# Two hybrid layers on one core: accumulate in PSUM, use ACT's own SiLU and GELU, and normalise one softmax on ACT

## The reference

```
def hybrid_layer(x, ...):
    z = rms_norm(x, norm1_g) @ w_in                    # 1024 -> 9984
    ya = silu(ga) * group_norm(retention(rotary(q), rotary(k), v)) * gn_g
    u  = a * sigmoid(gate)                             # conv branch
    yb = silu(layer_norm(causal_depthwise_conv31(u, conv_w) + conv_b))
    u, v = split(gelu(zc)); yc = u * (ws @ layer_norm(v) + b_s)
    p  = softmax over [scores + bias, sink]            # 8 heads of 64, window 128
    yd = p @ v
    mix = sum_n sigmoid(gate_n) * (y_n @ w_branch[n])  # 4 branches, 512 -> 1024
    x  = x + mix @ w_out
    gt, up = split(rms_norm(x, norm2_g) @ w_ffn_in)    # 1024 -> 2 x 2816
    return x + (silu(gt) * up) @ w_ffn_out
```

## Time and profile before

| | us |
|---|---|
| median of 3 runs | 2426.42 (2425.41 to 2430.86) |
| the profiled execution, its own time | 2424.03 |
| its span, first to last instruction | 2422.7 |
| PE busy | 2232.2 |
| DVE busy | 1631.0 |
| ACT busy | 1193.9 |
| POOL busy | 877.8 |

### The profile page before, as it was taken

How to read it: one execution, slowest core, us unless ns; L and a number is a source line. 1 busy time by engine, 2 the same in 40 slices (tenths; PEclk the granted TensorE clock), 3 DMA queues, 4 the chain that set the end, 5 groups by cost and what they waited for, 6 DMA issues and landing times.

```text
span 2422.7 us, 38114 instructions
## 1 busy us (share of the span) xinstructions
PE 2232.2 (92%) x15186; PEld 2068.3 (85%) x15186; DVE 1631.0 (67%) x2519; ACT 1193.9 (49%) x2040; POOL 877.8 (36%) x477
## 2 busy tenths in 40 slices
PE   8888889999999789999997798999999699898999
PEld 8887879999999678888886697889988588787997
DVE  6768742778544986666658789586655968777664
ACT  5546444454444975554552454535444255545443
POOL 5554457777200950000034474440004546442000
PEclk9999999999999999999998898899999899999999
DMA  6443445655556026666653344345664435334665
GB/s 222 131 122 112 133 152 178 183 162 179 179 185 184 12 76 194 192 194 195 194 175 126 121 144 131 105 141 163 184 190 145 131 106 156 112 116 150 183 186 160
DMA packets 102931, 369.59 MB, mean 153 GB/s; under 512 B 11362, under 2 KB 13794, under 8 KB 102116
## 3 DMA queue, kind: packets, MB, share of 16 engines
q1 hardware_dynamic: 102756, 367.15, 49.3%
HBM read 364.49 MB, written 2.62 MB: 152 GB/s over the span
## 4 chain that ended last, share of the span: by engine, by line
PE 62%; DVE 28%; ACT 5%; issue 3%; DMA 2%; POOL 1%; SPq 0%; DVEq 0%; ACTq 0%
PE stream_bank L530 10%; PE stream_bank L531 10%; PE stream_bank L532 10%; PE side_bank L530 9%; PE side_bank L531 9%; PE side_bank L532 9%; DVE conv_out L2030 6%; DVE first_hot L1970 2%; DVE unit_lo L1568 2%; DVE experts L1960 2%; ACT unit_hi L1048 1%; PE side_bank L592 1%; DVE S L1638 1%; DVE gates L1673 1%; POOL unit_lo L2302 1%
## 5 line engine op out<-in xcount | busy, mean ns | idle before, releaser
L2302 POOL TENSOR_TENSOR unit_lo<-raw,unit_hi 128x1024 fp32r<-128x1024 f32 (+1 forms) x305 | 754.0, 2481 | 519.1 <-ACT unit_hi L1048 518.8
L1048 ACT ACTIVATE unit_hi<-raw 128x1024 fp32r<-128x1024 f32 (+1 forms) x678 | 707.2, 1045 | 189.9 <-PE side_bank L532 82.6
L1568 DVE TENSOR_TENSOR unit_lo<-raw,unit_hi 128x1024 fp32r<-128x1024 f32 x373 | 459.3, 1232 | 390.6 <-ACT unit_hi L1048 390.0
L530 PE MATMUL stream_bank<-hT_hi,unit_hi 128*128 128x256 f32 x1672 | 501.4, 300 | 7.4 <-DVE unit_lo L1568 6.9
L531 PE MATMUL stream_bank<-hT_lo,unit_hi 128*128 128x256 f32 x1672 | 483.3, 289 | 0.0
L532 PE MATMUL stream_bank<-hT_hi,unit_lo 128*128 128x256 f32 x1672 | 482.5, 289 | 0.0
L530 PEld LDWEIGHTS stream_bank<-hT_hi,unit_hi 128*128 128x128 f32 x1672 | 332.2, 199 | 17.2 <-DVE unit_lo L1568 7.3
L531 PEld LDWEIGHTS stream_bank<-hT_lo,unit_hi 128*128 128x128 f32 x1672 | 331.9, 198 | 2.1
L532 PEld LDWEIGHTS stream_bank<-hT_hi,unit_lo 128*128 128x128 f32 x1672 | 330.9, 198 | 0.0
L530 PE MATMUL stream_bank<-h2T_hi,unit_hi 128*128 128x256 f32 x1152 | 327.4, 284 | 2.6 <-DVE unit_lo L1568 2.5
L531 PE MATMUL stream_bank<-h2T_lo,unit_hi 128*128 128x256 f32 x1152 | 326.7, 284 | 0.0
(11 more groups left out here) (354 smaller groups left out, 4260.6 us busy)
## 6 DMA issues: line engine op xcount, KB each, us to landing
raw<-in_peer_u_dram SPq DMA_DIRECT2D x128, 512.0 KB, 3.6
raw<-in_peer_v_dram SPq DMA_DIRECT2D x128, 512.0 KB, 3.6
raw<-in_gate_dram SPq DMA_DIRECT2D x64, 512.0 KB, 3.6
raw<-in_gt_dram SPq DMA_DIRECT2D x44, 512.0 KB, 3.6
raw<-in_up_dram SPq DMA_DIRECT2D x44, 512.0 KB, 3.7
raw<-in_ffn_out_dram SPq DMA_DIRECT2D x44, 512.0 KB, 4.2
raw<-in_branch_dram SPq DMA_DIRECT2D x32, 512.0 KB, 3.6
raw<-in_w_gate_dram SPq DMA_DIRECT2D x24, 512.0 KB, 3.6
```

Of the source, the lines that this page charges most:

```text
L530: mm(out, l.hi, r.hi, start=start, stop=False)
L1048: activation(k.unit_hi[n % SPLIT_SLOTS][:, 0:w], k.raw[n % RAW_SLOTS][:, 0:w], ACT.Copy).then_inc(k.sem("unit_hi"), 1)
L1568: V.tensor_tensor(k.unit_lo[s][:, 0:w], k.raw[n % RAW_SLOTS][:, 0:w], k.unit_hi[s][:, 0:w], ALU.subtract).then_inc(unit_lo, 1)
L2302: G.tensor_tensor(k.unit_lo[s][:, 0:w], k.raw[n % RAW_SLOTS][:, 0:w], k.unit_hi[s][:, 0:w], ALU.subtract).then_inc(k.sem("unit_lo_pool"), 1)
```

## The change

- **Convolution taps.** The sum so far is kept in `side_bank`4, in one half of the bank for even groups and the other for odd ones; only the last tap writes `cv` in SBUF. The factor one half of the gate's sigmoid moves into the 124 columns of taps (one small instruction a layer).
- **Rotation.** The product with the sines is written back into its bank; the add reads it there. The chunks use `side_bank`3 and 2 in turn, and the bank is given back after the add, one round later. `rope_tmp2` isn't used any more.
- **Gate products.** For three of the four branches the product stays in its stream bank and the add reads it there.
- **SiLU and GELU.** The evictions of `ga`, `gv` and `gu` apply ACT's function, the convolution's SiLU is one ACT instruction with the layer norm's scale and bias; the polynomials, tanh steps and multiplies go, and with them some rounds in which the side generators only waited.
- **Softmax of the window attention.** DVE stops after the inverse; ACT multiplies by it.

The diff, cut to its core:

```diff
 # PE: head
-        pe.wait_ge(k.sem("normed"), s.number + 1)
+        if s.kind == "swa":
+            pe.wait_ge(k.sem("normed_act"), s.number - HEADS_MIXER + 1)
+        else:
+            pe.wait_ge(k.sem("normed"), s.number + 1)
...
 # PE: retention
-                bank = take(SIDE + 3, (name("rot"), c))
+                bank = take(SIDE + 2 + (c + 1) % 2, (name("rot"), c))
...
 # ACT: head
+        if s.kind == "swa":
+            act.wait_ge(k.sem("inverse"), s.number - HEADS_MIXER + 1)
+            for i, (a, kn) in enumerate(s.where):
+                last = activation(s.S[:, a:a + kn], s.S[:, a:a + kn], ACT.Identity, scale=s.den[:, i:i + 1])
+            last.then_inc(k.sem("normed_act"), 1)
...
 # ACT: convolution
-                activation(k.t2[:, 0, :], k.cv[:, i, :], ACT.Tanh, scale=0.5).then_inc(k.sem("conv_tanh"), 1)
-                act.wait_ge(k.sem("conv_silu"), KM * l + i + 1)
-                split_hi(k.ys.hi[:, 4 + i, :], k.cv[:, i, :], "conv_hi", 0.5)
+                own.then(activation(k.cv[:, i, :], k.cv[:, i, :], ACT.Silu, scale=k.col(name("cln_g"), i),
+                                    bias=k.col(name("cln_b"), i)))
+                split_hi(k.ys.hi[:, 4 + i, :], k.cv[:, i, :], "conv_hi")
...
 # ACT: main
-                evict(name("ga"), i, k.ga[:, i, :])
+                evict(name("ga"), i, k.ga[:, i, :], ACT.Silu)
...
-                    evict_token_major(name("gv"), k.gv, 512)
+                    evict_token_major(name("gv"), k.gv, 512, ACT.Gelu_apprx_tanh)
...
 # DVE: head
-        own.then(V.reciprocal(s.den, s.den))
-        for i, (a, kn) in enumerate(s.where):
-            last = V.tensor_scalar(s.S[:, a:a + kn], s.S[:, a:a + kn], s.den[:, i:i + 1], None, ALU.mult)
-        last.then_inc(k.sem("normed"), 1)
+        if s.kind == "swa":
+            V.reciprocal(s.den, s.den).then_inc(k.sem("inverse"), 1)
...
 # DVE: convolution
-                cv = k.cv[:, i, :]
-                own.then(V.tensor_scalar(cv, k.cu[:, i, 0:TOKENS], w(0), k.col(name("conv_b2"), i), ALU.mult, ALU.add))
+                sums = bank[:, i % 2 * TOKENS:(i % 2 + 1) * TOKENS]
+                own.then(V.tensor_scalar(sums, k.cu[:, i, 0:TOKENS], w(0), k.col(name("conv_b2"), i), ALU.mult, ALU.add))
                 for j in range(1, TAPS2 - 1):
-                    own.then(V.scalar_tensor_tensor(cv, k.cu[:, i, j:j + TOKENS], w(j), cv, ALU.mult, ALU.add))
+                    own.then(V.scalar_tensor_tensor(sums, k.cu[:, i, j:j + TOKENS], w(j), sums, ALU.mult, ALU.add))
...
-                gelu_cubic(tmp, u, "gelu_u_cubic")
-                yield
-                yield
-                dve.wait_ge(k.sem("gelu_u_tanh"), n)
-                own.then(V.scalar_tensor_tensor(u, tmp, 1.0, u, ALU.add, ALU.mult))
...
 # DVE: retention
-                V.tensor_tensor(k.rqk[:, c, :], k.rqk[:, c, :], k.rope_tmp2[:, :], ALU.add).then_inc(k.sem("rotated"), 1)
-                dve.wait_ge(k.sem("rotated"), 8 * l + c + 1)
+                V.tensor_tensor(k.rqk[:, c, :], k.rqk[:, c, :], turned(c), ALU.add).then_inc(k.free[SIDE + 2 + (c + 1) % 2], 1)
...
+                dve.wait_ge(k.sem("rot_mm"), 8 * l + c + 1)
+                own.then(V.tensor_tensor(turned(c), turned(c), k.ret_sin, ALU.mult))
                 if c:
                     add(c - 1)
-                dve.wait_ge(k.sem("rot_mm"), 8 * l + c + 1)
-                V.tensor_tensor(k.rope_tmp2[:, :], k.bank[SIDE + 3][:, 0:TOKENS], k.ret_sin, ALU.mult).then_inc(
-                    k.free[SIDE + 3], 1)
-                dve.wait_ge(*k.over[name("rot"), c])
...
 # DVE: main, branches
-                    gated_sum(gate, k.bank[k.bank_of[label]], label, 2)
+                    product = k.bank[b][:, :].rearrange("p (a t) -> p a t", a=2)
...
-                    if 0 < place < BRANCHES2 - 1:
-                        own.then(V.tensor_tensor(total, total, gate, ALU.add))
+                    if place == 0:
+                        gated_sum(gate, k.bank[b], label, 2)
+                    else:
+                        dve.wait_ge(unit_mm, U[label] + 1)
+                        own.then(V.scalar_tensor_tensor(product, gate, 1.0, product, ALU.add, ALU.mult))
+                        V.tensor_tensor(total, total, product, ALU.add).then_inc(k.free[b], 1)
+                        dve.wait_ge(*k.over[label])
```

More of the change, by code:

```diff
@@ L1060, in evict, with evict_token_major @@
         activation(dst, k.bank[b][:, 0:TOKENS], func, **kw).then_inc(k.free[b], 1)
-    def evict_token_major(key, dst, width):
+    def evict_token_major(key, dst, width, func=ACT.Copy):
         for t in range(TILES):
             act.wait_ge(unit_mm, at.unit)
-            activation(dst[:, t, :], k.bank[SIDE + t][:, 0:width], ACT.Copy).then_inc(k.free[SIDE + t], 1)
+            activation(dst[:, t, :], k.bank[SIDE + t][:, 0:width], func).then_inc(k.free[SIDE + t], 1)
     def norm_stats(name, x, ready, junk):
@@ L1427, in retention_head @@
                 yield
[L1428 to L1431 removed]
             yield
             act.wait_ge(*k.over[name("ret_turn"), h])
[L1434 removed]
+            split_hi(k.ys.hi[:, h, :], k.ga[:, h, :], "ret_hi")
             yield
@@ L1498, in main @@
             for i in range(KM):
-                evict(name("gu"), i, k.gu[:, i, :])
+                evict(name("gu"), i, k.gu[:, i, :], ACT.Gelu_apprx_tanh)
                 yield
@@ L1635, in head @@
             dve.wait_ge(*k.over[label])
-        own.then(V.reciprocal(s.den, s.den))
-        for i, (a, kn) in enumerate(s.where):
-            last = V.tensor_scalar(s.S[:, a:a + kn], s.S[:, a:a + kn], s.den[:, i:i + 1], None, ALU.mult)
-        last.then_inc(k.sem("normed"), 1)
+        if s.kind == "swa":
+            V.reciprocal(s.den, s.den).then_inc(k.sem("inverse"), 1)
+        else:
+            own.then(V.reciprocal(s.den, s.den))
+            for i, (a, kn) in enumerate(s.where):
+                last = V.tensor_scalar(s.S[:, a:a + kn], s.S[:, a:a + kn], s.den[:, i:i + 1], None, ALU.mult)
+            last.then_inc(k.sem("normed"), 1)
         yield
@@ L2001, in layer @@
             pass
-        own.then(V.memset(k.cu[:, :, 0:TAPS2 - 1], 0.0))
+        V.memset(k.cu[:, :, 0:TAPS2 - 1], 0.0)
+        taps = k.col(name("conv_w2"), 0, TAPS2 * KM)
+        own.then(V.tensor_scalar(taps, taps, 0.5, None, ALU.mult))
         if l == 0:
@@ L2022, in convolution @@
         def convolution():
+            bank, mean, var = k.bank[SIDE + 4], k.t2[:, 0, :], k.t2[:, 1, :]
             for i in range(KM):
@@ L2033, in convolution @@
                 j = TAPS2 - 1
-                V.scalar_tensor_tensor(cv, k.cu[:, i, j:j + TOKENS], w(j), cv, ALU.mult, ALU.add).then_inc(
+                V.scalar_tensor_tensor(k.cv[:, i, :], k.cu[:, i, j:j + TOKENS], w(j), sums, ALU.mult, ALU.add).then_inc(
                     k.sem("conv_taps"), 1)
@@ L2038, in convolution @@
             yield
-            bank, mean, var = k.bank[SIDE + 4], k.t2[:, 0, :], k.t2[:, 1, :]
             dve.wait_ge(k.sem("conv_mm"), 2 * l + 1)
@@ L2057, in convolution @@
                 u, n = k.cv[:, i, :], KM * l + i + 1
[L2058 to L2063 removed]
+                V.tensor_tensor(u, u, var, ALU.mult).then_inc(k.sem("conv_normed"), 1)
+                dve.wait_ge(k.sem("conv_hi"), n)
+                V.tensor_tensor(k.ys.lo[:, 4 + i, :], u, k.ys.hi[:, 4 + i, :], ALU.subtract).then_inc(k.sem("conv_lo"), 1)
                 yield
@@ L2166, in retention_head @@
             ga = k.ga[:, h, :]
-            dve.wait_ge(k.sem("ret_tanh"), g + 1)
+            dve.wait_ge(*k.over[name("ga"), h])
             dve.wait_ge(k.sem("ret_turned"), g + 1)
-            own.then(V.scalar_tensor_tensor(ga, k.ret_s[:, :], 1.0, ga, ALU.add, ALU.mult))
             V.scalar_tensor_tensor(ga, b[:, 0:TOKENS], k.col(name("gn"), h), ga, ALU.mult, ALU.mult).then_inc(
                 k.free[SIDE + 2], 1)
-            half_lo(k.ys.lo[:, h, :], ga, k.ys.hi[:, h, :], (k.sem("ret_hi"), g + 1), "ret_lo")
+            dve.wait_ge(k.sem("ret_hi"), g + 1)
+            V.tensor_tensor(k.ys.lo[:, h, :], ga, k.ys.hi[:, h, :], ALU.subtract).then_inc(k.sem("ret_lo"), 1)
             yield
@@ L2220, in main @@
                 dve.wait_ge(*k.over[label])
-                own.then(V.tensor_scalar(cu, cu, 0.5, None, ALU.mult))
                 yield
@@ L2373, in gating_norm @@
             for t in range(TILES):
-                for _ in range(6):
+                for _ in range(3):
                     yield
```

56 lines of the change are left out of this document (13 added, 43 removed).

## The result

| | before | changed | predicted |
|---|---|---|---|
| median, us | 2426.92 (4 runs, 2425.41 to 2430.86) | 2315.12 (4 runs, 2314.54 to 2315.47) | 2323 (2294 to 2367) |
| ratio | | 0.9541 (0.9527 to 0.9555) | 0.957 |
| span of the profiled execution | 2422.7 | 2313.9 | |

What follows compares the result with a forecast made beforehand. In the mixing stages PE waits for DVE, whose SBUF instructions are held while POOL makes weight units. Seven terms sum to 103.5 us, taking 2424.0 to 2320.5; with 2.4 for the runs' median, 2323 (2294 to 2367).

Steps and rivals of the forecast that it cites:

- (7): Clock shortfall of the two mixing stages outside the rotation: half of 38 us comes back, a gain of 19 us.
- Taps: All 248 convolution taps of both layers: 0.49 us each with the sum in PSUM, bounds 0.41 and 0.87.
- (1): Rotation, 8 rounds a layer: 54.0 and 47.0 us become 37.8 and 32.7, a gain of 30.5 us.
- Case C: Taps still held, or dear through PSUM, at 0.87 us: only 42 us gained, 2384 us; chance 0.05.
- (2): First retention head, L916: PE's wait of 9.1 us in each layer all gone, a gain of 18.2 us.
- (3): Transpose of the first retention head, L926: PE's wait falls from 5.9 to 1 us a layer, gain 9.8 us.
- (4): Window attention, L622: PE's waits of 22.2 us fall to 7 us, a gain of 15 us.
- (5): Convolution's sums, L838: PE's wait of 3.1 us gone, counted as a gain of 3 us.
- (6): Last gated sums: DVE's 4.6 us a unit becomes 2.8, gaining 8 of PE's 9.3 us of waits.
- Rival A: Mixing stages: ACT becomes the late engine, table loads standing ahead of evictions; 59.7 us gained, 2367 us; chance 0.20.
- Rival B: Mixing stages: nearly nothing is left of PE's waits; 139.5 us gained, 2287 us; chance 0.12.
- D: Convolution taps: writing PSUM costs over 1.04 us each, so the kernel is slower; at 1.2 us, 2466 us; chance 0.04.

Runs made afterwards that it cites:

- the fastest version: The changed kernel with the rotation one round later, bias tables in side_bank0 and 1, and the remaining held lines moved to PSUM: 2298.68 us.

## Why the prediction was right, and where it was not

The mechanism is shown: a VectorE instruction with two input tensors, both in SBUF, stands until GpSimd's running weight unit has ended. Taking GpSimd away (held time 218.6 to 9.7 us), halving its instruction (longest tap 2.69 to 1.58) and moving the tensors to PSUM (longest tap 0.49) all remove or shorten it, and the ends of held taps follow the ends of GpSimd's instructions to 0.01 us. The Trainium skill names this contention, without its length, in "GPSIMD Engine Reference", section "Key points": the engine shares its SBUF interfaces with VectorE, in contention with instructions that have two SBUF inputs or run in a 2-port mode. The trace agrees, also on the second kind: the softmax multiply has one tensor input and was held for up to 2547 ns. The forecast's wording, "two tensors in SBUF", was thus too narrow for the multiply by a column. "All tensors in SBUF", as in some expectations above, is too wide: the 12 maxima of the softmax (TENSOR_REDUCE) that began while GpSimd's unit ran in the kernel before took 0.29 and 0.41 us like the other 20, and a reciprocal on 128x256 1.745 us as the rest. Neither touches the sums.

The forecast counted waits and clock apart, but the rotation as a whole. So do these lines: the fall of PE's idle time in the table's stretch, and under (7) that of its busy time.

- Taps: 488 ns against the 0.49 taken; the bounds 0.41 and 0.87 were wide on both sides. The Trainium skill, "VectorE: DVE Perf Modes", section on the TRN2 errata, has a fixed surcharge for a PSUM source (an estimated 0.065 us a tap); it doesn't show: 489 ns against a median of 485 in SBUF.
- (1) Rotation, 30.5: measured 29.6, of which 8.9 are busy time. The taps alone give 25.9 of it, the rotation's own edit alone nothing (103.8 against 103.7), and without the taps all is lost. Case C's "half of (1)" was wrong, and so were the expectations for the rotation alone and the taps taken back, for one reason: held taps fill the round, whichever line the hold is seen on.
- (2) L916, 18.2: 18.2.
- (3) L926, 9.8: 6.4. 5.4 us of waits are left, not 2. The forecast blamed what would stay on the square root's table load; the add of epsilon on two numbers (L2129), held for up to 2.1 us, stands ahead of it, and with that add gone 3.1 are left.
- (4) Window attention, 15: 14.9. One wait of 4.0 us a layer is left, the forecast's 7 us nearly. With the held lines put into PSUM it goes, but the gating's bank then makes PE wait as long.
- (5) The convolution's end, 3: 7.0. The forecast read only L838's longest wait. The trace of before has 4.9 and 5.6 us of waits in these stretches, among them 3.3 for a weight unit of VectorE's own (L1568) and 3.0 for the variances of the q and k norms (L2179).
- (6) Last branch, 8: 12.9 of idle time, and 4.5 of busy time at a granted clock of 1.00 before and after. The step "PE waits behind it with 4.7 + 4.6 us" took one line of PE's waits; 2.8 at L592 and 0.8 for the fourth unit stood behind the same held sums. This term was the one most wrong in size.
- (7) Clock, 19 outside the rotation: PE's busy time fell by 31.6 us in the stretches, 8.9 in the rotation, 4.5 in the last branch, and 18.2 in the four between, which lost 39.1 us of clock before and lose 10.2 now. "Half of 38" had no better reason than its bounds; that it came so near is luck.

In all 111.7 in the stretches, less 2.9 us that the profiled run of the changed kernel was later before them, gives 108.8. Against the forecast's 103.5 the terms are 9.4 too small in (6) and 4.0 in (5), 3.4 too large in (3) and about 1 each in (1) and (7). Rival A had L1107 right as a line that PE waits for, but at 8.0 us, not 44; ACT is busy for 196 of 380 us. What spoke for A is small: evictions through SiLU and GELU took 0.38 us, as plain ones. Rival B's 2287 wasn't reached even by the fastest version. C and D fell with the tap's 0.49.

Open is why half-width units on GpSimd also gain 9.8 us in the first block, and whether the changed kernel gains from VectorE doing all weight units; with 26 us held and 188 to be added, the numbers here speak against it.
